# The second recurrent tile's scan behind the scores' decay products, in a two-branch streaming layer

## What is computed

```
conv_out, conv_state = _causal_conv(z[..., :c0], conv_prev, conv_w, conv_b)
# recurrent branch, per channel
r = sigmoid(x @ w_r + b_r);  i = sigmoid(x @ w_i + b_i)
log_a = -8 * r * softplus(-lam);  a = exp(log_a)
u = sqrt(-expm1(2 * log_a)) * (i * x)
h[t] = a[t] * h[t-1] + u[t]                      # scan over the frames
# matrix memory, 4 heads of 256
s = einsum('bhtd,bhsd->bhts', q, k) * exp(dlog - m_t)     # scores times decay
num = s @ v + inter * (C @ q);  den = sum(s) + inter * (n . q)
C_new = decay * C + (v * wk)^T @ k;  n_new = decay * n + wk . k
merged = sigmoid(g_a) * (lru_y @ w_pa) + sigmoid(g_b) * (m_y @ w_pb)
x = x + merged @ w_out;  x = x + moe(rmsnorm(x))
```

## Time and profile before

| what | value |
|---|---|
| median of 3 runs | 1031.45 us (1026.59 to 1033.77) |
| the profiled execution | 1030.39 us, span 1028.5 us |
| TensorE busy (products) | 961.6 us, 93% |
| VectorE busy | 674.8 us, 66% |
| ScalarE busy | 548.5 us, 53% |
| GpSimd busy | 268.1 us, 26% |
| chain that ended last | TensorE 73%, VectorE 13%, ScalarE 3% |
| granted TensorE clock, mean | 0.98 |

### The profile page before, as it was taken

One profiled execution on the slowest core, in us unless ns is written; L12 is line 12 of the kernel. 1 busy time (PEld: TensorE's weight loads), 2 busy tenths in 40 slices (PEclk: granted clock), 3 DMA queues, 4 the chain that ended last, 5 costly groups with the idle time before them and its releaser, 6 DMA issues.

```text
span 1028.5 us, 16729 instructions
## 1 busy us (share of the span) xinstructions
PE 961.6 (93%) x5973; PEld 848.2 (82%) x5973; DVE 674.8 (66%) x867; ACT 548.5 (53%) x610; POOL 268.1 (26%) x184
## 2 busy tenths in 40 slices
PE   5999899999999999899999999939899999999984
PEld 3999789879988987799999986827788888888873
DVE  5496659758875976521111114389999999898966
ACT  5645525724542573333333323357787887878742
POOL 1014204323330432234433443004211101010161
PEclk9999999999999999999999999969999999999998
DMA  9552122313222221132332269129999999999986
GB/s 286 189 174 62 47 72 63 90 38 92 72 56 72 61 61 41 42 103 82 85 99 82 82 210 307 74 104 304 401 405 415 412 415 413 414 414 413 378 217 167
DMA packets 146455, 193.17 MB, mean 188 GB/s; under 512 B 14456, under 2 KB 91662, under 8 KB 146292
## 3 DMA queue, kind: packets, MB, share of 16 engines
q1 hardware_dynamic: 139290, 166.32, 46.6%
q0 software_dynamic: 4656, 16.21, 5.1%
q10 hardware_dynamic: 2474, 10.18, 2.5%
HBM read 172.91 MB, written 19.77 MB: 187 GB/s over the span
## 4 chain that ended last, share of the span: by engine, by line
PE 73%; DVE 13%; issue 5%; ACT 3%; SPq 2%; DMA 2%; DVEq 1%; POOL 0%; ACTq 0%; POOLq 0%
PE PJ L472 60%; DVE MEM L1769 2%; DVE MEM_R L2038 2%; PE NM L1346 2%; PE MS L1364 2%; PE PJ L1282 2%; PE MS L1315 1%; PE MS L1548 1%; DVE MEM L1872 1%; SPq L619 1%; DMA MEM<-in_x_prompt_dram 1%; PE NM L1487 1%; PE MS L1338 1%; PE NM L1579 1%; DVE MEM_R L1679 1%
## 5 line engine op out<-in xcount | busy, mean ns | idle before, releaser
L472 PE MATMUL PJ<-MEM_R 128*128 128x272 f32 (+2 forms) x5016 | 799.8, 320 | 12.4 <-DVE MEM_R L2160 3.1
L472 PEld LDWEIGHTS PJ<-MEM_R 128*128 128x128 f32 x5016 | 719.2, 190 | 74.9 <-issue 12.3
L694 POOL TENSOR_TENSOR MEM_R<-RAW,MEM_R 128x1024 fp32r<-128x1024 f32 x72 | 177.7, 2475 | 346.4 <-ACT MEM_R L843 346.4
L2038 DVE TENSOR_TENSOR MEM_R<-CHUNK,MEM_R 128x2048 fp32r<-128x2048 f32 x100 | 225.5, 2295 | 16.2 <-ACT MEM_R L1104 14.9
L1104 ACT CAST MEM_R<-CHUNK 128x2048 fp32r<-128x2048 f32 x100 | 189.4, 1912 | 13.8 <-PE PJ L472 10.3
L843 ACT CAST MEM_R<-RAW 128x1024 fp32r<-128x1024 f32 x81 | 84.2, 1048 | 122.6 <-DMA RAW<-in_w_pb_dram 40.7
L1942 DVE TENSOR_TENSOR MERGED<-PJ,MEM 128x544 f32<-128x544 f32 x14 | 10.1, 725 | 132.5 <-PE PJ L472 132.5
L774 POOL COPY MEM<-MEM 128x1 uint32 (+1 forms) x16 | 21.2, 1323 | 224.7 <-PE MS L1548 224.7
L1769 DVE SCALAR_TENSOR_TENSOR MEM<-MEM 128x548 f32<-128x548 f32 x72 | 58.9, 818 | 8.5 <-DVE MEM L1767 0.9
L1113 ACT CAST MEM_R<-MS 128x1024 fp32r<-128x1024 f32 x17 | 17.3, 1016 | 34.3 <-PE MS L1548 34.3
L900 ACT COPY MEM<-PJ 128x272 f32<-128x272 f32 x24 | 9.1, 377 | 41.3 <-PE PJ L472 41.3
(11 more groups left out here) (335 smaller groups left out, 909.3 us busy)
## 6 DMA issues: line engine op xcount, KB each, us to landing
CHUNK<-in_w_gate_dram SPq DMA_DIRECT2D x34, 1024.0 KB, 8.2
CHUNK<-in_w_up_dram SPq DMA_DIRECT2D x34, 1024.0 KB, 9.8
CHUNK<-in_w_down_dram SPq DMA_DIRECT2D x34, 1024.0 KB, 8.6
RAW<-in_w_in_dram SPq DMA_DIRECT2D x56, 512.0 KB, 3.7
expert_rows<-MEM ACTq DMA_DIRECT2D x15, 512.0 KB, 6.0
expert_rows<-MEM SPq DMA_DIRECT2D x10, 512.0 KB
RAW<-in_w_pa_dram SPq DMA_DIRECT2D x8, 512.0 KB, 3.6
RAW<-in_w_pb_dram SPq DMA_DIRECT2D x8, 512.0 KB, 3.6
```

The lines of the kernel that those rows point to most:

```text
L472: ins = pe.matmul(out, w(a), x(b), start=first and n == 0, stop=last and n == 2)
L694: tt(lo, raw[slot], hi.bitcast(F32), ALU.subtract).then_inc(lo_done, 1)
L2038: tt(moe_hl[c][1], moe_raw[c], moe_hl[c][0].bitcast(F32), ALU.subtract).then_inc(chunk_lo[c], 1)
```

## The change

In `lru` the last step is no longer waited for, and the root product with its two scans becomes a function of its own, `lru_scan`, with the wait for `root_ready`. For tile 0 it is called where it stood. For tile 1 it is called in `probabilities`, behind the five decay products, and a wait for `lru_done` keeps the weighted keys from overwriting the gate buffer that the scan reads. The number of VectorE's steps in a head is unchanged.

```diff
--- before.py
+++ after.py
@@ -1782,7 +1782,11 @@
                 dve.wait_ge(decay_ready, hd * CT + (c + 1))
                 st.link(tt(r, tmp[:, 2, :], tmp[:, 2, :], ALU.mult))
                 stt(r, r, 1.0, tmp[:, 3, :], ALU.add, ALU.mult).then_inc(poly_ready, 1)
-                st.link(tt(u, u, xc[:, c, :], ALU.mult))
+                st.do(tt(u, u, xc[:, c, :], ALU.mult))
+
+            def lru_scan(hd, c):
+                u = ri[c][:, 1, :]
+                st.wait()
                 dve.wait_ge(root_ready, hd * CT + (c + 1))
                 st.link(tt(u, u, tmp[:, 3, :], ALU.mult))
                 y = line(lru_y[:, ds(hd * CT + c, 1), :])
@@ -1802,6 +1806,7 @@
                 conv(hd, 4)
                 conv(hd, 5)
                 lru(hd, 0)
+                lru_scan(hd, 0)
                 lru(hd, 1)
 
             def probabilities(hd):
@@ -1812,6 +1817,9 @@
                     dve.wait_ge(masked, hd * J + (j + 1))
                     d = dp[:, j, P * j:LP] if j < JP else dp[0:LS, j, 0:LS]
                     emptied(tt(d, b[0:d.shape[0], 0:d.shape[1]], d, ALU.mult))
+                lru_scan(hd, 1)
+                st.wait()
+                dve.wait_ge(lru_done, hd * CT + CT)
                 for j in range(J):
                     n = rows_of[j]
                     b = misc(hd, 6 + j // 2)
```

## The result

The changed kernel took 1047.23 us, median of 4 runs (1046.34 to 1047.98), against 1032.61 (1026.59 to 1033.81, 4 runs) for the kernel before: a ratio of 1.0156, 95% interval 1.0126 to 1.0187. It is 1.6% slower. Its profiled execution has a span of 1044.4 us, 15.9 more than before's. In the rows of the changed kernel the root product is L1791, the scans are L1793 and L1794, the copy L1814, the decay products L1819 and the weighted keys L1826.

The account below looks back on a forecast made before the run. TensorE, busy nearly all the time outside the four seams, was taken as the bound, so its seam costs count fully: 1030.39 + 7.6 (order of work) + 4.6 (clock) = 1042.6 us, range 1033 to 1047.

Parts of the forecast that it names:

- Gain in front: Before score unit 2: earlier copy of the old state removes TensorE's wait, 2.26 us at seam 0, 0.34 at seams 1 and 2.
- Loss behind, with GpSimd's hold: Unit 8 starts later because GpSimd's subtractions hold the moved operations: +1.3, +2.2, +2.2, +1.9 us over the seams, 7.6 net.
- The clock: Behind unit 8: TensorE's idling lowers its clock, costing 1.5 us at seam 0, 1.2 at seams 1 and 2, 0.7 at seam 3.
- The discount for a part that falls into the wait: Clock cost at seams 1 and 2 taken as 1.2 us, not 1.5, since slow time may fall in TensorE's wait.
- Passing through: Inside each head: VectorE's stretch moves with TensorE and absorbs nothing, so the seams' delay reaches the kernel's time.
- The base: Starting time of the forecast: the profiled execution's 1030.39 us, 1.1 below the median 1031.45.
- GpSimd not in the way: Rival at the seams: subtractions do not hold the moved step; +1.5 us and +3 for the clock, 1032 to 1035; chance 0.17.
- absorbed: Rival inside the heads: TensorE's slack takes up the late unit 8, seam 0 keeps its gain, 1026.6 us; chance 0.06.
- seam 3 dearer: Rival at seam 3: ScalarE's held cast delays the recurrent branch's split, 2 to 4 us more, 1045 to 1049; chance 0.10.

Follow-up runs that it names:

- the first experiment: Changed kernel, but GpSimd waits for the second tile's scan before subtracting the next head's weights: 1037.3 us, ratio to before 1.0066.
- filler: Changed kernel plus six, three, three and two unread 128x512 TensorE products ahead of unit 8 at seams 0 to 3: 1038.56 us, ratio 1.0075.
- the second profile: Changed kernel run again with no edit, six runs: 1047.24 us, ratio to the kernel before 1.0156.
- the kernel with two fillers: Changed kernel plus two unread 128x512 TensorE products per head between units 7 and 8: 1042.88 us, ratio to before 1.0121.

## Why the prediction was wrong

The direction, the mechanism and each seam's delay came out; the time, 1047.2, lies above 1042.6 and just outside the range that ended at 1047.0.

- *Gain in front:* right. The copy came early enough at every seam, and the wait of 2.26 us and the old fall of the clock went.
- *Loss behind, with GpSimd's hold:* right, 7.9 us for 7.6. Seam 0 +1.55 for 1.3, seams 1 and 2 +2.36 for 2.2, seam 3 +1.64 for 1.9. Both holds at seam 0 and the single one at seams 1 and 2 are there; taking GpSimd away gave 5.4 us back, for 6.1 in the sum. Two small things were off: at seams 1 and 2 the root product took 1.69 us where the prediction asked for 2 or more, since it was issued 0.2 us later and ended by the same subtraction; and the hand-over was 0.32 us at seams 0 to 2, with GpSimd in the way or without it (the row of L1827 in the first experiment), and didn't show at seam 3.
- *The clock:* this is the step that failed, "a fall costs 1.5 us, none costs 0", together 4.6 us and at most 6. It cost 5.1 us in one profile, 8.4 in the other and 8.7 by the medians with and without filler. Of the eight passages behind unit 8 in the two profiles three cost 1.3 to 1.5 us, four 2.2 to 2.4 and one nothing. I had priced one fall, the 1.5 us at 430.73, and made it the upper end. What the sum lacked is how long the lower level lasts. It lasted 3.4 us in the two falls that the prediction read and 6.8 us in five of the seven at the changed seams; the trace of before could have warned, with a stretch of 20.5 us at the lower level from 673 us on. The discount for a part that falls into the wait was right in kind: at seam 0 of the first profile 3.7 of the 6.8 us did, and that fall cost 1.3 us where the others of its length cost 2.2 to 2.4. What sets the length and the start of a low stretch stays open; the same wait of 3.6 us at seam 1 was followed by 3.4 us in one execution and by 6.8 in the other.
- *Passing through:* right. With the clock held up, 7.9 us of delay made the stretch 7.9 us longer; the seams of the changed kernel lie 97.0 and 94.6 us apart, for 94.1 and 90.7.
- *The base:* the sum was made on the profiled execution's 1030.39, and the runs of before had a median of 1031 to 1032.6; this is another 0.6 to 2.2 us.
- *Rivals:* GpSimd not in the way falls by the held rows; absorbed falls by the 7.9 us that passed through; seam 3 dearer falls, since ScalarE's cast started 6.8 us late and TensorE's product at 421.53 did not wait for it.

In sum 7.9 + 8.4 = 16.3 us for the stretch of the second profile, against 7.6 + 4.6 = 12.2. The lock rule of the Trainium skill (SBUF — State Buffer, "SBUF: two separate sides") agrees with the held rows at 116 and 213 us too, and with the unheld one at 404 us.

## What to carry to other kernels

When a step moves on one engine, look at what the other engines do at its new place, not only at who waits for it: two-input operations of VectorE that were free beside an idle GpSimd were held for up to 2 us beside its subtraction. Where a move shortens one wait of TensorE and lengthens another, count both the wait and the clock behind it, and don't take the few falls that the trace happens to show for the upper end of the price: read from the granted clock how long the lower level lasted, and how much of it fell on work. And look for the cheap form of the gain: here nine small operations, 2 us in all, in front of the copy made the wait at the first seam, and an idle gap of 3.5 us ahead of them had room for them (3.4 us in the trace, a gain that the medians leave open).

## What was not expected of the hardware

The clock fell behind idle 1.92 us at seam 1 of the kernel with two fillers and did not fall behind 2.18 us at seam 3 in the first profile of the changed kernel, though it did in the second; nor did it fall behind 2.66 us at seam 2 with GpSimd waiting. The length of one idle gap did not decide it. Nor did a longer low stretch need a longer gap: behind 3.6 us at seam 1 it lasted 3.4 us or 6.8, and at seam 1 of the first profile it began 0.8 us after TensorE had taken up its work again. Useless products ahead of the late unit made the changed kernel 8.7 us faster. A scan over 32 frames, 0.26 us by itself, took 2.30 us because GpSimd's subtraction began while the long scan in front of it ran.
